# Order of values and turns on TensorE in the attention steps of a fused NSA and GLA decoder layer

## The reference

```python
def attend(q, k, v, bias, mask):
    s = jnp.einsum('...qgrd,...kgd->...grqk', q, k) * scale + bias
    p = masked_softmax(s, mask)
    return jnp.einsum('...grqk,...kgd->...qgrd', p, v), p
```

## Time and profile before

| | |
|---|---|
| runs | 1370.34, 1368.97, 1368.87 us; median 1368.97 |
| profiled execution | 1367.36 us, span 1365.6 us |
| mean granted TensorE clock | 0.990 |
| busy, share of the span | TensorE 96%, weight loads 86%, VectorE 46%, ScalarE 45%, GpSimd 11% |

### The profile page before, as it was taken

The page is one execution under the profiler, slowest core; times in us unless marked ns, Lnnn a source line. Parts: engine busy times, 40 slices in busy tenths (PEclk is TensorE's granted clock), DMA queues, the critical chain, the costliest instruction groups (busy, mean ns, idle before and its releaser), DMA issues.

```text
span 1365.6 us, 23608 instructions
## 1 busy us (share of the span) xinstructions
PE 1304.6 (96%) x9533; PEld 1175.7 (86%) x9533; DVE 623.8 (46%) x1387; ACT 620.1 (45%) x1068; POOL 148.1 (11%) x185
## 2 busy tenths in 40 slices
PE   5999998998999999999999999999989989999998
PEld 4999998998988889999898889888866778999876
DVE  5202144644843444433333333466578766453342
ACT  6212335542456545665556545765457532221121
POOL 2100001102300000000000300313010270000000
PEclk9999999999999999999999999999999999999999
DMA  7251453521522211222222222554345746552331
GB/s 205 63 169 41 118 148 102 146 68 41 99 63 64 64 45 56 64 79 63 62 60 55 68 63 63 178 172 135 101 163 184 259 144 192 153 151 68 107 118 61
DMA packets 156908, 145.27 MB, mean 106 GB/s; under 512 B 27360, under 2 KB 141360, under 8 KB 156736
## 3 DMA queue, kind: packets, MB, share of 16 engines
q1 hardware_dynamic: 154016, 135.33, 32.8%
q0 software_dynamic: 2784, 8.43, 2.0%
HBM read 105.88 MB, written 41.88 MB: 108 GB/s over the span
## 4 chain that ended last, share of the span: by engine, by line
PE 55%; DVE 3%; ACT 2%; issue 1%; POOL 1%; DMA 0%; DVEq 0%; SPq 0%; ACTq 0%
PE ps L240 31%; PE ps L2533 7%; PE ps L1645 4%; PE ps L1679 4%; PE ps L1661 3%; PE ps L1694 1%; POOL oL L2582 1%; PE ps L2441 1%; DVE S L2644 1%; PE ps L2409 1%; PE ps L1764 1%; PE ps L2541 1%; PE ps L2445 1%; PE ps L2500 0%; DVE bsum L1386 0%
## 5 line engine op out<-in xcount | busy, mean ns | idle before, releaser
L240 PE MATMUL ps<-hH,wH 128*128 128x352 f32 (+1 forms) x1320 | 440.1, 333 | 7.3 <-DVE stg L375 3.0
L240 PE MATMUL ps<-hH,wL 128*128 128x352 f32 (+1 forms) x1320 | 426.5, 323 | 0.0
L240 PE MATMUL ps<-hL,wH 128*128 128x352 f32 (+1 forms) x1320 | 425.4, 322 | 0.0
L240 PEld LDWEIGHTS ps<-hH,wH 128*128 128x128 f32 (+1 forms) x1320 | 248.1, 188 | 34.7 <-issue 26.5
L240 PEld LDWEIGHTS ps<-hL,wH 128*128 128x128 f32 (+1 forms) x1320 | 249.3, 189 | 2.2 <-issue 1.9
L240 PEld LDWEIGHTS ps<-hH,wL 128*128 128x128 f32 (+1 forms) x1320 | 248.5, 188 | 0.3
L227 DVE TENSOR_TENSOR wL<-w_raw,wH 128x1024 fp32r<-128x1024 f32 (+1 forms) x70 | 86.8, 1242 | 133.2 <-ACT wH L219 133.2
L2000 DVE CUSTOM_DVE_ANT_0 sP<-ps,dist,stat 128x256 f32<-128x256 f32 (+3 forms) x116 | 58.6, 542 | 179.2 <-issue 109.4
L360 ACT ACTIVATE stg<-ps 128x352 f32<-128x352 f32 x132 | 61.0, 462 | 116.6 <-PE ps L240 116.0
L219 ACT ACTIVATE wH<-w_raw 128x1024 fp32r<-128x1024 f32 (+1 forms) x70 | 73.4, 1049 | 70.7 <-issue 39.8
L2197 ACT ACTIVATE pPT<-ps 128x512 f32<-128x512 f32 x74 | 44.1, 595 | 134.1 <-PE ps L1661 132.2
(11 more groups left out here) (390 smaller groups left out, 2054.8 us busy)
## 6 DMA issues: line engine op xcount, KB each, us to landing
w_raw<-in_w_in SPq DMA_DIRECT2D x61, 512.0 KB, 3.9
p_spill<-stg SPq DMA_DIRECT2D x132, 176.0 KB, 1.8
zt<-p_spill SPq DMA_DIRECT2D x24, 528.0 KB, 4.9
w_raw<-in_w_in SPq DMA_DIRECT2D x17, 256.0 KB, 3.8
gvT<-p_spill SPq DMA_DIRECT2D x8, 528.0 KB, 5.4
x_all<-in_x_prompt SPq DMA_DIRECT2D x8, 512.0 KB, 9.3
m_raw<-in_w_branch_b SPq DMA_DIRECT2D x8, 512.0 KB, 5.5
xr<-in_x_prompt SPq DMA_DIRECT2D x8, 512.0 KB, 3.5
```

What stands on the lines that cost most here:

```text
L240: mm = nc.tensor.matmul(ps[0:t.m, bank, 0:NF], w[:, c % 2, t.m * k:t.m * k + t.m], x[n][:, k, :], start=(k == 0 and i == 0), stop=(k == t. ...
```

## The change

On TensorE, in the steps 1 to 48, `values(m - 1)` is issued ahead of `transposes(m)` and behind the units. In steps 49 to 65 the order stays. No instruction is added or taken out, and every wait stays with its group.

```diff
                 slot(t, 0)
+                if 1 <= m < M0:
+                    values(m - 1)
                 transposes(m)
-                if m >= 1:
+                if m >= max(M0, 1):
                     values(m - 1)
                 slot(t, 1)
```

## The result

The changed kernel took 1376.32 us (median of 5 runs, 1374.66 to 1379.12), the kernel before 1368.97 us (5 runs, 1367.22 to 1370.34). The ratio is 1.0045, with a 95% interval from 1.0031 to 1.0059: slower by 0.3 to 0.6%. The profiled execution has a span of 1374.6 us (1365.6 before) at a mean clock of 0.989.

The account below looks back on a forecast made before the run. It took TensorE's own list to bound the main part; 0.152 us a step for one more weight-shape change, times 48, less 0.34 us, gave +7.0 us on the median 1369.0: 1376.0 us, range 1373.3 to 1378.8.

Parts of the forecast that it names:

- The bound: Main part: TensorE's own list is the path, busy 442.9 of 446.0 us, so its start-to-start times set the time.
- Leaving a unit into values: Last unit matmul of a step, now followed by another weight shape: 0.095 us more, bounds 0 to 0.10.
- Entering the turns: Turns now follow values of another weight shape instead of units: 0.057 us more a step, bounds 0 and 0.11.
- The exp's 0.34 us: Turns of step 26 wait for an exp; values ahead of them would cover it, saving 0.34 us.
- The sum: Main part: 0.152 us a step times 48 is +7.3 us, less 0.34, gives +7.0 us.
- The cover: Room for later copies: 0.8 us left ahead of each of 11 spreads, 0.14 us for VectorE's copy in step 26.
- ScalarE's wait for the turns: ScalarE waits for turns in 46 steps, 132.2 us in all; expected to rise by some 50 us.
- The free join (1): Prefetched weight loads hide the price of a shape change: -0.3 us, 1368.7 us, chance 0.05; entering price only: 1371.4, chance 0.02.
- the dearer one (2): Entering costs the turns as much as it costs a unit: +9.7 us, 1378.7 us; chance 0.05.
- late copies (4): Later copies make ScalarE late for spreads or VectorE late for values: 3.3 us more, 1379.3 us; chance 0.03.
- hidden waits for exps (3): Turns wait for exps more often than shown and values fill it: with 12 steps -4.9 us, 1364.1 us; chance 0.02.
- A give-back in the tail (5): A shorter path in the tail takes back 2 to 3 us of the 7: 1373.5 us; chance 0.05.

Follow-up runs that it names:

- U S T V: Main steps reordered to units, scores, turns, values, against the kernel before (units, turns, values, scores): 1371.41 us, ratio 1.0030 to 1.0067.
- the split values: Kernel before with each step's values in two halves, one ahead of the scores and one behind: 1372.90 us, ratio 1.0001 to 1.0039.
- values in pairs: Order units, turns, scores, values, with two steps' values issued together in every second step, against the kernel before: 1364.75 us, ratio 0.9942 to 0.9971.
- waits at the head: Kernel before, its order kept, with the two waits of the values also put ahead of the turns: 1370.24 us, ratio 0.9979 to 1.0014.
- 128*128 values: Changed kernel, order and waits kept, with the values' weights made 128 columns wide: 1403.32 us, ratio to the kernel before 1.0237 to 1.0327.
- scores ahead of values: Main steps reordered to units, turns, scores, values, against the kernel before: 1360.07 us, ratio 0.9944 to 0.9978.

## Why the prediction was right

**The bound.** TensorE's own list is the path of the main part: the changed kernel, U S T V and the split values, with the same matmuls, moved the turns row by what their joins cost, less the waits that shrank, to within 1 us.

**The terms.** Leaving a unit into values, which no row of before showed, was taken at 0.095 and measures 0.10 (0.26 against 0.16). Entering the turns: 0.057 taken, 0.06 measured (1.03 against 0.97). Values 1.02, as taken. The exp's 0.34 us came back. The sum was +7.0 for 48 steps; the turns row, which holds 47 of the 48 joins of unit and values, says +6.9. That the two medians, 1376.32 - 1368.97 = 7.35, come so near is in part luck: the interval of the ratio reaches from 4.2 to 8.1 us, and one stretch of low clock is worth 1.6.

**The cover.** No new wait of TensorE came up, neither for a spread nor for VectorE's copy in step 26, from the timeline of the changed kernel:

```profile
650.78 0.69 DVE L2012 COPY pPT<-ps 128x512 f32<-128x512 f32 x1
```

It ends at 651.47, 0.19 us ahead of the values that need it (651.66, the change of shape included). The values in pairs show what a missed cover costs: 0.2 us a step.

**One size was off.** ScalarE's wait for the turns should have risen by some 50 us; it rose by 28, from 132.2 to 159.9. Waits of ScalarE, 415 to 868 us in the changed kernel:

```profile
ACT pPT L2199 <- PE ps L1661: 159.9, 47, 9.1
...
ACT tmp L2199 <- PE ps L1694: 21.3, 11, 1.9
ACT stg L360 <- PE ps L240: 17.6, 9, 4.6
```

Ahead of a spread it waited 1.0 us less each time (21.3 in place of 32.5 in the earlier trace rows), since the spread had moved by 0.15 only, and ahead of take-outs (L360) 17.6 in place of 26.9. The three together rose by 7, from 191.6 to 198.8, which is what the main part got longer. I had reckoned one wait of a chain that meets TensorE at several points. It had no weight in the sum.

**The rivals.** The free join (1) and the dearer one (2) are out by the timeline; late copies (4) by the waits and by the run with waits at the head; hidden waits for exps (3) because the one wait in step 26 is all that went. A give-back in the tail (5) isn't seen, though clock stretches of 1.6 us each would hide one of a microsecond: it stays open.

"TensorEngine Tiling (Array Packing)" of the Trainium skill (Key Properties: changing the tiling mode drains the engine) says nothing of the price. The traces agree that such a change costs: 0.10 us for leaving in each order tried. "TensorE: Matmul & The Clock Gate" of the Trainium skill (Part 2, LDWEIGHTS) describes that the next weight load is pulled ahead of matmuls in flight. In these traces that holds between groups of one shape (the loader's 0.3 us ahead of the turns with 128*128 values) and not across a change (7.9 us).

## What to carry to other kernels

In a loop like this one, where TensorE is hardly ever idle, the order of its groups is priced by the joins: count how often the weight shape changes in the loop, and read start to start, not TensorE's printed idle time, which shows nothing of it. Work put ahead of a wait pays only for the time that the wait really lasts, here 0.34 us in 48 steps, against 0.15 us in each for a join broken. To gain, put groups of one shape side by side, and the group that another engine waits for first: scores ahead of values gave 0.4%, and of the row's 3.8 us nearly half comes from spreads that follow values, the rest from shorter waits. And check what the group that moves back releases: values in pairs saved 3.2 us of joins and lost 1.8 where ScalarE came later for it. A row that runs from one kind of group to its last one is a fair measure only if it holds the same groups in both kernels.

## What the runs showed that I had not expected

The 3.4 us at half clock behind the 2.6 us wait at 497 us was missing in two kernels with the same wait (values 128*128, and waits at the head), so it is not fixed by the wait. In the kernels whose wait was 2.0 us or less it didn't show either. What decides it stays open.
